# Gate buffers for the last tile of a recurrent block, and a new hand-out of score tiles in the prompt attention

## What is computed

```python
u = h @ w_in                                   # recurrent block
gate_br, x_br = jnp.split(u, 2, axis=-1)
xc, conv_new = _causal_dwconv(x_br, conv_buf, conv_w, conv_b)
r = jax.nn.sigmoid(xb @ wa + ba)               # block-diagonal, xb is xc in 16 blocks
i = jax.nn.sigmoid(xb @ wx + bx)
log_a = -RG_C * r * jax.nn.softplus(-lam)
a = jnp.exp(log_a)
b = jnp.sqrt(-jnp.expm1(2.0 * log_a)) * (i * xc)
_, hs = lax.associative_scan(_lin_combine, (a, b), axis=1)
y = (jax.nn.gelu(gate_br) * hs) @ w_out
...
s = jnp.einsum('bqhd,bkhd->bhqk', qblk, k) * scale   # attention, per block of 128 queries
s = s + cq - ck                                       # sums of log forget gates
p = jax.nn.softmax(jnp.where(mask, s, -jnp.inf), axis=-1)
o = jnp.einsum('bhqk,bkhd->bqhd', p, v)
```

## Time and profile before

| | |
|---|---|
| median of three runs | 3179.97 us (3177.86 to 3180.47) |
| the profiled execution, whole | 3177.67 us |
| its span | 3176.2 us |
| TensorE busy | 3006.1 us, 95% |
| VectorE busy | 1392.2 us, 44% |
| GpSimd busy | 1135.6 us, 36% |
| ScalarE busy | 868.9 us, 27% |
| recurrent block | about 100 to 475 us of the span |
| prompt attention | about 1801 to 2097 us |

### The profile page before, as it was taken

The page is one execution under the profiler, slowest core; times in us unless marked ns, Lnnn a source line. Parts: engine busy times, 40 slices in busy tenths (PEclk is TensorE's granted clock), DMA queues, the critical chain, the costliest instruction groups (busy, mean ns, idle before and its releaser), DMA issues.

```text
span 3176.2 us, 48823 instructions
## 1 busy us (share of the span) xinstructions
PE 3006.1 (95%) x19182; PEld 2812.3 (89%) x19182; DVE 1392.2 (44%) x2011; ACT 868.9 (27%) x1464; POOL 1135.6 (36%) x569
## 2 busy tenths in 40 slices
PE   6999989899999999998999888889899999999996
PEld 4878779899999999998999766658899999999996
DVE  6454672543434434445103265642453434344445
ACT  3233440331212212122212255541241212121122
POOL 1222236433333333332333355533333333333331
PEclk9999999999999999999999899999999999999998
DMA  6666222111111111111534454674111111111111
GB/s 224 245 221 233 73 86 67 52 47 47 40 46 40 46 46 40 46 41 47 168 130 177 136 135 97 180 285 163 40 49 45 46 40 46 41 45 46 40 46 69
DMA packets 100217, 294.60 MB, mean 93 GB/s; under 512 B 15008, under 2 KB 16416, under 8 KB 99856
## 3 DMA queue, kind: packets, MB, share of 16 engines
q1 hardware_dynamic: 86368, 243.53, 23.1%
q10 hardware_dynamic: 13744, 49.61, 4.5%
HBM read 253.00 MB, written 40.10 MB: 92 GB/s over the span
## 4 chain that ended last, share of the span: by engine, by line
PE 41%; issue 30%; POOL 10%; ACT 2%; DVE 1%; DMA 1%; POOLq 0%; SPq 0%; ACTq 0%; DVEq 0%
PE PS L664 33%; POOL WH L593 6%; POOL WL L596 4%; PE PS L972 2%; PE PS L955 2%; PE PS L939 1%; PE PS L940 1%; ACT PX L1397 1%; DMA WRAW<-in_wstream 1%; DMA KB<-in_cache_k 0%; ACT PT L1387 0%; PE PS L986 0%; DVE X L2022 0%; PE PS L1018 0%; PE PS L941 0%
## 5 line engine op out<-in xcount | busy, mean ns | idle before, releaser
L593 POOL TENSOR_TENSOR WH<-WRAW,ZERO 128x1024 fp32r<-128x1024 f32 x212 | 417.9, 1971 | 1788.2 <-ACTq L1105 1273.7
L664 PE MATMUL PS<-HH,WH 128*128 128x342 f32 (+1 forms) x3120 | 693.4, 330 | 16.1 <-ACT RS L1190 11.0
L664 PE MATMUL PS<-HL,WH 128*128 128x342 f32 (+1 forms) x3120 | 692.6, 330 | 0.0
L664 PE MATMUL PS<-HH,WL 128*128 128x342 f32 (+1 forms) x3120 | 690.4, 330 | 0.0
L664 PEld LDWEIGHTS PS<-HH,WH 128*128 128x128 f32 x3120 | 552.0, 189 | 24.7 <-issue 21.8
L596 POOL TENSOR_TENSOR WL<-WRAW,WH 128x1024 fp32r<-128x1024 f32 x212 | 550.8, 2598 | 16.6
L664 PEld LDWEIGHTS PS<-HH,WL 128*128 128x128 f32 x3120 | 554.4, 189 | 1.6
L664 PEld LDWEIGHTS PS<-HL,WH 128*128 128x128 f32 x3120 | 555.5, 189 | 0.2
L1795 DVE SCALAR_TENSOR_TENSOR FC<-FU,FCW,FC 128x1026 f32<-128x1026 f32 x96 | 239.9, 2499 | 572.6 <-ACT FC L1249 572.6
L664 PE MATMUL PS<-AH,WH 128*128 128x342 f32 (+1 forms) x1152 | 256.2, 330 | 7.1 <-DVE AL L1813 4.9
L664 PE MATMUL PS<-AH,WL 128*128 128x342 f32 (+1 forms) x1152 | 254.9, 329 | 0.0
(11 more groups left out here) (252 smaller groups left out, 3546.8 us busy)
## 6 DMA issues: line engine op xcount, KB each, us to landing
WRAW<-in_wstream SPq DMA_DIRECT2D x212, 512.0 KB, 3.5
MS<-in_mod_w SPq DMA_DIRECT2D x96, 512.0 KB, 7.1
KB<-in_cache_k SPq DMA_DIRECT2D x32, 512.0 KB, 8.8
VB<-in_cache_v SPq DMA_DIRECT2D x32, 512.0 KB, 8.4
K<-k_split SPq DMA_DIRECT2D x48, 256.0 KB
Q<-q_split SPq DMA_DIRECT2D x48, 256.0 KB
out_kv<-STG ACTq DMA_DIRECT2D x16, 545.0 KB, 3.1
MU<-in_mod_w SPq DMA_DIRECT2D x16, 512.0 KB, 12.5
```

Source lines behind the costliest of these rows:

```text
L593: pool.tensor_tensor(WH[:, u, :], WRAW[:, u, :], ZERO[:].broadcast_to([P, UNIT]), ALU.add).then_inc(hi.sem, 1)
L664: mm = pe.matmul(PS[:, o:o + hi - lo], lhs(n), rhs[:, k, lo:hi], start=first and n == 0 and m == 0, stop=last and n == len(kts) - 1 and m ...
```

## The change

It has two independent parts.

The last tile of the recurrent block, tile 9, gets gate buffers of its own for the two gates, the root and the exponential: YG slot 9 (which is otherwise first written by g9), slots 3 and 2 of XC (tiles 7 and 6, no longer read) and the head of RU (no longer read once tile 9 is convolved). Before the first sigmoid of tile 9 ScalarE waits for `conv_free`, that is for the convolution of tile 9, instead of for the recurrence of tile 8. The count of `pair_free` is made up behind the list, where ScalarE waits for both recurrences at once.

In the attention AHEAD hands out one score tile in each of the 8 steps of an even group; in the 6 steps of an odd one it hands out one in each of the first four and two in each of the last two. Since the last step of a group now has score tiles, their exponentials and reciprocals come in step 0 of the next group: `tiles_behind` gives ScalarE and VectorE the tiles of the step before, across the border of a group.

```diff
-AHEAD = ((0, 0, 2, 2, 4, 4, 5, 5), (0, 0, 1, 2, 3, 3, 4, 4))
+AHEAD = ((0, 1, 2, 3, 4, 5, 6, 7), (0, 1, 2, 3, 4, 4, 5, 5))
...
+    def gate_buffers(j):
+
+        if j < LATE[1]:
+            return RS1[:], RI1[:], RQ1[:], RA1[:]
+        return YG[:, 9, :], XC[:, 3, :], XC[:, 2, :], RU[:, 0:T]
...
+    def tiles_behind(g, i):
+        if i:
+            return [(g + 1, a, e) for a, e in tiles_ahead(g, i - 1)]
+        return [(g, a, e) for a, e in tiles_ahead(g - 1, STEPS[(g - 1) % 2] - 1)] if g else []
...
         def both_gates(j):
-            act.wait_ge(pair_free.sem, pair_free.next())
-            rs, ri, rq, ra = RS1[:], RI1[:], RQ1[:], RA1[:]
+            if j < LATE[1]:
+                act.wait_ge(pair_free.sem, pair_free.next())
+            else:
+                act.wait_ge(conv_free.sem, conv_free.next())
+            rs, ri, rq, ra = gate_buffers(j)
...
-        act.wait_ge(pair_free.sem, pair_free.next())
+        act.wait_ge(pair_free.sem, pair_free.next(2))
         act.dma_start(O["rst"], RST[:]).then_inc(S["rst_out"], 16)
...
-                for a, e in tiles_ahead(g, i - 1):
-                    exps(g + 1, a, e)
+                for of, a, e in tiles_behind(g, i):
+                    exps(of, a, e)
...
         def recurrence(j):
-            rs, ri, rq, ra = RS1[:], RI1[:], RQ1[:], RA1[:]
-            hs = HS8[:] if j == LATE[0] else XC[:, 2, :] if j == LATE[1] else rq
+            rs, ri, rq, ra = gate_buffers(j)
+            hs = HS8[:] if j == LATE[0] else rq
...
-                for a, e in tiles_ahead(g, i - 1):
-                    inverse(g + 1, a, e)
+                for of, a, e in tiles_behind(g, i):
+                    inverse(of, a, e)
```

## The result

| | before | after |
|---|---|---|
| median (lowest to highest), 4 runs each | 3178.91 us (3176.68 to 3180.47) | 3159.31 us (3157.55 to 3160.64) |
| span of the profiled execution | 3176.2 us | 3156.1 us |

What follows compares the result with a forecast made beforehand. TensorE, busy 95% of the span, was taken as the bound, so only its gaps and lower-clock time could be won. Recurrent -7.0 and attention -18.9 gave -25.9 us: 3151.8 profiled, 3154.1 as median, range 3146 to 3168.

Steps and rivals of the forecast that it cites:

- recurrent term: Recurrent block's end: earlier gates of tile 9 save 7.9 us, clock 0.3, new charge 1.2; sum -7.0 us, bounds -10 and -4.
- attention term: Attention: the new order of score tiles removes TensorE waits for exponentials; -18.9 us, bounds -13 and -25.
- rival B: Output projection: GpSimd's splits and VectorE's YL tiles give the recurrent gain back, -2 instead of -7, 3159 us; chance 0.07.
- clock term: Unit g8: a shorter idle time leaves TensorE less time at the lower clock; -0.3 us, between 0 and -2.0.
- charge of +1.2 us: Output projection: TensorE waits for GpSimd's late split of the second output weight; +1.2 us, bounds 0 and 2.5.
- step account: Attention pairs replayed step by step from TensorE's starts: even groups gain 0.8 us, odd 1.9; a pair lasts 31.5 us.
- rival A: Attention: close waits at odd groups' ends lower TensorE's clock, costing 10 to 17 us, time near 3167; chance 0.20.
- deduction of 0.5 us: Attention, group 1: 0.5 us taken off the gain because VectorE also fills buffers there.
- deduction of 1.0 us: Attention, group 13: 1.0 us taken off the gain because VectorE's scans hold the copies up either way.
- E: Recurrent block: ScalarE's new wait or another reader of tile 9's buffers ends as late as before; 3161 us, chance 0.05.
- C: Attention: waits only move, each single score waiting for its predecessor's exponential; attention gives 0, 3173 us; chance 0.06.
- D: Attention: clock stays at the lower level for long parts; half of each pair low gives 3258 us; chance 0.04.

Runs made afterwards that it cites:

- the exponential first: Against after, ScalarE takes exponentials ahead of the copy in steps 4 and 5 of odd groups and step 0 of even ones: 3140.78 us, ratio 0.9885.
- all three edits: After plus rows of ones written earlier, exponentials ahead of the copy in three steps, and low parts of Y ahead of tile 8's product: 3135.07 us, ratio 0.9865.
- the low parts moved: Against after, VectorE makes the low parts of Y of tiles 0 to 4 ahead of the product of tile 8: 3159.09 us, ratio 0.9945.

## Why the prediction was right, and where its steps were off

**Right in direction and range; the time came out 5.2 us above the forecast.** The recurrent term was right as a sum by luck, since two errors in it offset each other; the attention term was too large by 7.6 us. The measured 3159.3 is also what rival B names (3159): the number alone does not choose between them, the experiments do.

**Recurrent block, -7.0 forecast, -7.3 in the trace, -6.8 with the part alone.** The start of g8 was right to 0.3 us (424.42 forecast, 424.16 measured; wait 3.1 and 3.12), and so was VectorE's start on tile 9 (431.9 and 431.59). Two terms were mis-sized:
- The clock term was taken as -0.3 between 0 and -2.0. It was -1.9 in this execution: granted 1.00 in 425 to 430 where it had been 0.62, so TensorE took 12.1 us for g8 and not 14.0 (the forecast's "until ScalarE had it at 446.50" is 14.2 us by its row). Six kernels have the new recurrent part and the same 3.12 us of idle time. In three of them (after, the recurrent part alone, the exponential first) g8 took 12.1 us; in the other three the clock fell up to 1.5 us into it and g8 took 13.6. So the -0.3 was right for half of them.
- The charge of +1.2 us was put on GpSimd's split of the second output unit, said to be late because ScalarE takes g9 from PSUM late. ScalarE did take it late (452.27; forecast 452.5), but GpSimd had been released at 448.58, just behind TensorE's last matmul of g9 (448.46). The acknowledgement is an instruction of ScalarE's queue, and the queue was 3.7 us ahead of the work. The split was in time. What TensorE waited for instead were the YL tiles, 0.39 and 1.63 us.

Why these were late is one event with the clock. A g8 at full clock ends early and releases GpSimd's first split early, ahead of VectorE's 8-column product and scan of tile 9; both then wait for GpSimd (1.74 and 4.49 us), and the YL tiles start at 446.38. In the three kernels in which the clock fell, the split came behind the start of the scan, the two took 0.17 and 2.43 us, the YL tiles started at 444.2 to 444.6, and TensorE waited for none. From the start of g8 to the first residual it took 49.6 us in the three kernels with the full clock, 48.6 in the three others and 48.9 before. So the full clock saved 1.5 us in g8 and cost 2.5 behind it. This is read from six traces; no edit forced the one case or the other. That the five YL tiles themselves took 10.01 us beside the second split (7.37 before, without one) adds to their lateness; with the earlier start 9.06 us did no harm.

The Trainium skill (SBUF — State Buffer, section "Who interferes with whom") has VectorE instructions with two SBUF inputs and GpSimd instructions that read SBUF exclude each other, whoever is first making the other wait; the rows agree in both directions: an 8-column product took 1.74 us instead of 0.17 where GpSimd was first, and GpSimd's first half of a split 4.03 us instead of 2.71 where the scan was first. The forecast had the end of the recurrence right (444.4; measured 444.31) but did not carry the delay on to the YL tiles, though rival B named them.

**Ordinary pairs, -2.7 each forecast.** The step account held: 31.5 us forecast, 31.60 measured, the waits 0.93, 0.71 and 0.61 us at the three places named (1.1, 0.94 and 0.88 forecast, from start to start). The failed step is the one that took the clock as given and moved its risk wholly into rival A. Two of the five pairs lost 1.4 and 1.5 us again at the lower level, 3.0 us together. Rival A had the mechanism and the size of one event right (1.7 us), and the number of events wrong: two, not six and more. The Trainium skill (TensorE: Matmul & The Clock Gate, section "A second HAM failure mode: psum-queue depth-cycling") describes the clock going up and down where many small idle spots part groups of matmuls; with the waits at 0.17 us the granted clock stayed at 1.00 from 1850 to 2020, and with them it fell in two of five pairs here, in three of five with the attention part alone and with the odd row alone. The prediction read the ordinary group of before as evidence against it; that row stood for waits at other places and distances than the new order has, and so was weaker evidence than it was taken for.

**The first pair, -2.9 forecast, -0.5 measured.** The prediction's view of this stretch was the same step account with a deduction of 0.5 us "where VectorE also fills buffers". What it did not ask is when the loads for group 2 are issued. They are issued behind VectorE's rows of ones, which the table doesn't move, and they were early enough before, so that no wait of the old trace pointed at them. The rows of ones themselves did show in it, as the wait of 3.21 us for the copy behind them, which the forecast passed over. The experiment with the rows moved took 7.2 us off this stretch: the waits of 4.35 and 2.79 us went, one of 0.95 came, and the remaining 1 us was not traced.

**Groups 12 and 13, -1.7 forecast, -0.1 measured.** The deduction of 1.0 us for VectorE's scans was too small: the wait for the copy behind them is 2.03 us and not 1.04, a second one of 1.15 follows, and 2040 to 2050 ran at 0.66. All kernels with the new odd row show the same 2.02 or 2.03 us. The scans were not moved in any run, so that they are the cause is read from VectorE's timeline (1.21 and 1.68 us of scans directly ahead of the late copy) and not shown. The last pair gave 0.7 of the 0.8 forecast.

**Behind the attention** 1.3 us more were gained than the forecast has. The first three matmuls of the output products took 0.76 us in after and 1.27 in before, each behind a wait of 1.99 us, so the clock has a part in it. Of the ten profiled kernels only before and the one with all three edits have 1.27 us there, so it looks like chance and not like the change; how much of the 1.3 us it explains was not traced.

**Rivals.** A came true in part (3 of the 10 to 17 us). B and E fell with the recurrent part alone, C with the pairs of 31.60 us, D with the granted clock.

**What stays open.** Why some pairs lose their clock and others not, with identical waits (every second one in after; the first and the third of five with the low parts moved); why one pair of the even row alone lost it; whether the scans of group 13 are worth moving.

## What to carry to other kernels

A wait for a consumer with free time is a question of its order first: ScalarE was busy for 19 us of a pair of 31.6, and swapping two of its instructions in three places brought 18.5 us, nearly as much as the whole change. When a stage is made faster, look for what its speed does not move (loads issued behind another engine's set-up work, and the gap between a transfer's landing and its use), since the gain ends there without a wait in the old profile to tell of it. Several waits of less than 1 us close together have a second price in the clock behind them, here 1.4 us on top of 2.2 in two or three pairs of five, so it pays to take them away rather than to spread them differently. An engine that finishes sooner also releases others sooner: here a unit that ended 1.5 us earlier let a split in ahead of a scan, and the stage took 1.0 us longer.

## What the runs showed of the hardware

- After the same idle time of 3.12 us TensorE stayed at full clock in three of six kernels, fell to the lower level at once in one (first three matmuls 1.25 us instead of 0.73) and fell about 1 to 1.5 us later in two. After 10.96 us idle it was 1.25 us in all four kernels with the old recurrent part.
- A semaphore that ScalarE's queue increments ahead of an activation came 3.7 us ahead of that activation (448.58 and 452.27), while the activations queued before it were still running; it followed TensorE's last matmul of the unit (448.46).
- Four rows of ones took 0.68 us each where GpSimd stood idle and 0.95 to 2.16 us where it was at work.
- Whether GpSimd's split or VectorE's scan started first decided which was stretched: the split's first half took 2.71 and the scan 4.49 us with the split ahead, 4.03 and 2.43 with the scan ahead.
- The odd row of the table alone saved 1.06 us a pair while the clock held and lost 0.5 to 2.6 us a pair against before when it did not: the sign of an edit changed with the clock.
